# Six small re-orderings in a two-layer mixture-of-experts decoder trunk on one Trainium2 core

## The reference

```python
def reference(x, c, ...):
    cond = silu(c)
    h = x                                     # 512 tokens, 1024 channels
    for layer in range(2):
        mod = cond @ w_ada[layer] + b_ada[layer]
        sh1, sc1, g1, sh2, sc2, g2 = split(mod, 6)
        u = rms_norm(h, norm_mix[layer]) * (1 + sc1) + sh1
        if layer == 0:
            q, k, v, bg, cg, xv = split(u @ w_in)
            attn = sliding_window_attention(q, k, v, sinks)   # 8 heads of 64, window 128
            conv = bg * conv3(cg * xv)
            mix = concat(attn, conv) @ w_out
        else:
            mix = multiscale_pool_mixer(u, w_pool, pool_scale)
        h = h + g1 * mix
        u = rms_norm(h, norm_ffn[layer]) * (1 + sc2) + sh2
        h = h + g2 * grouped_moe(u, ...)      # 16 experts in 4 groups
    return rms_norm(h, norm_final)

def grouped_moe(...):
    # a token picks the best one of 4 groups, then the best 2 experts inside that group
    for e in range(16):
        out += gates[:, e] * ((silu(t @ w_gate[e]) * (t @ w_up[e])) @ w_down[e])
```

## Time and profile before

| | us |
|---|---|
| median of 3 runs | 782.37 (781.77 to 783.32) |
| profiled execution | 781.47 |
| its span | 779.6 |
| PE busy | 677.0 (87%) |
| DVE busy | 346.9 (44%) |
| ACT busy | 167.8 (22%) |
| POOL busy | 112.9 (14%) |
| transfers | 204.27 MB, 262 GB/s in the mean |

### The profile page before, as it was taken

One profiled execution on the slowest core, in us unless ns is written; L12 is line 12 of the kernel. 1 busy time (PEld: TensorE's weight loads), 2 busy tenths in 40 slices (PEclk: granted clock), 3 DMA queues, 4 the chain that ended last, 5 costly groups with the idle time before them and its releaser, 6 DMA issues. The chain is left out here.

```text
span 779.6 us, 7210 instructions
## 1 busy us (share of the span) xinstructions
PE 677.0 (87%) x2441; PEld 355.9 (46%) x2441; DVE 346.9 (44%) x623; ACT 167.8 (22%) x422; POOL 112.9 (14%) x87
## 2 busy tenths in 40 slices
PE   4899989999899955999999999179299999999960
PEld 2455434444444453455455454069255544554520
DVE  2226698999952356222232231336643223222312
ACT  4101121322212322121122121046022211211212
POOL 0000001001210032012212220100201222122020
PEclk8899999999999965999999999779589999999995
DMA  8999989978870376488888988525606889898326
GB/s 267 314 387 373 360 292 325 340 243 300 273 267 22 141 276 249 176 314 335 310 314 337 333 301 314 190 109 173 270 27 224 333 319 322 312 347 313 113 35 231
DMA packets 59930, 204.27 MB, mean 262 GB/s; under 512 B 13510, under 2 KB 22878, under 8 KB 47612
## 3 DMA queue, kind: packets, MB, share of 16 engines
q1 hardware_dynamic: 45012, 183.62, 62.1%
q0 software_dynamic: 10096, 19.45, 10.2%
q10 hardware_dynamic: 4792, 0.82, 0.6%
HBM read 193.06 MB, written 27.30 MB: 283 GB/s over the span
## 5 line engine op out<-in xcount | busy, mean ns | idle before, releaser
L1541 PE MATMUL ps<-ring,work 128*128 128x512 f32 x384 | 170.1, 596 | 0.0
L1541 PEld LDWEIGHTS ps<-ring,work 128*128 128x128 f32 x384 | 73.3, 192 | 90.7 <-issue 90.5
L844 DVE SCALAR_TENSOR_TENSOR acc<-adaw,cond,acc 128x1024 f32<-128x1024 f32 x70 | 97.4, 1391 | 10.1 <-DMA adaw<-in_w_ada_dram 8.2
L531 POOL DMA_INDIRECT h_dram<-work x32 | 50.6, 1581 | 309.0 <-DVE work L1159 285.3
L1140 DVE TENSOR_TENSOR work<-work,ps 128x256 f32<-128x256 f32 x32 | 13.5, 421 | 177.9 <-ACT work L753 177.8
L1564 PE MATMUL psY<-ring,work 128*128 128x512 f32 x192 | 86.6, 594 | 1.2 <-ACT work L763 1.2
L1396 PE MATMUL psY<-xu,ring 128*128 128x512 f32 x192 | 86.0, 601 | 0.0
L1159 DVE SCALAR_TENSOR_TENSOR work<-psY,work,gbc 128x512 f32<-128x512 f32 x64 | 45.1, 746 | 74.4 <-PE psY L1564 74.4
L753 ACT ACTIVATE work<-ps 128x256 f32<-128x256 f32 x32 | 12.3, 384 | 271.6 <-PE ps L1541 271.6
L1396 PEld LDWEIGHTS psY<-xu,ring 128*128 128x128 f32 x192 | 35.9, 192 | 45.4 <-issue 45.3
L747 ACT ACTIVATE work<-psA,modc,scl 128x128 f32<-128x128 f32 x120 | 45.2, 457 | 51.7 <-PE psA L1531 51.7
(11 more groups left out here) (183 smaller groups left out, 641.0 us busy)
## 6 DMA issues: line engine op xcount, KB each, us to landing
adaw<-in_w_ada_dram SPq DMA_DIRECT2D x84, 512.0 KB, 5.3
ring<-in_w_gate_dram SPq DMA_DIRECT2D x24, 1024.0 KB, 4.8
ring<-in_w_up_dram SPq DMA_DIRECT2D x24, 1024.0 KB, 7.0
ring<-in_w_down_dram SPq DMA_DIRECT2D x24, 1024.0 KB, 11.4
xu<-in_w_gate_dram SPq DMA_DIRECT2D x8, 1024.0 KB, 4.9
xu<-in_w_up_dram SPq DMA_DIRECT2D x8, 1024.0 KB, 7.0
xu<-in_w_down_dram SPq DMA_DIRECT2D x8, 1024.0 KB, 11.0
work<-in_w_ada_dram SPq DMA_DIRECT2D x12, 512.0 KB, 10.4
```

The source lines that it names most:

```text
L531: pool.indirect_dma_start(out=h_dram[l], out_offset=bass.IndirectOffsetOnAxis(tok_i[:, e:e + 1], 0), in_=yrow[:, e % 2, :], in_offset=None ...
L844: dve.scalar_tensor_tensor(total, adaw[:, n % ABUF, :], cond[:, k:k + 1], total if k else brow[:, :], ALU.mult, ALU.add).then_inc(mac_step, 1)
L1541: ins = pe.matmul(gu_ps[j % 2][:, :].rearrange("p (a f) -> p a f", a=2), xgT[:, j % 2, k, :], w_gu(j % 4)[:, :, k, :], start=(k == 0), sto ...
```

## The change

- The ten small loads leave ACT's queue for the head of POOL's program, behind a wait for the third `first_read`.
- One dummy matmul at the start instead of three.
- The first modulation sum (`ada_total(0)`, `ada_out(0)`) stands ahead of the attention units instead of inside the first.
- `scores` and `attend` alternate between the two halves of the array.
- The last eight experts are taken in the order 8, 12, 9, 13, 10, 14, 11, 15: SP loads their weights in that order, and the table's columns follow. Neighbours are of different groups from there on, so from the eleventh scatter of a layer on, a scatter waits for the one before the last.
- SP's second round of expert loads is written out. The loads of layer 1's first three experts stand behind the loads of h.

```diff
             def summed(i):
 
                 if i < 2:
-                    return 0
+                    return max(i, 0)
                 return NPC if i == len(PLACES) - 1 else sum(PLACES[:i - LAG + 1]) // KD
...
                 load_expert(l, 3, 3)
-                with sp.Fori(1, E // 4) as i:
+                for j in range(4):
+                    load_expert(l, 4 + j, j)
+                with sp.Fori(2, E // 4) as i:
                     for j in range(4):
-                        load_expert(l, 4 * i + j, j)
-                if l == 0:
-                    for e in range(3):
-                        load_expert(1, e, e)
+                        load_expert(l, 4 * i + j, j, 2 * i + 4 + j // 2 + 4 * (j % 2))
                 overflow_sync(sp, l)
 
                 for j in range(2):
                     sp.wait_ge(y_out[j], 8 * E * (l + 1))
                 for t in range(T):
                     sp.dma_start(h[:, t, :], h_dram[l][t * P:(t + 1) * P, :]).then_inc(h_back[t], 16)
+                if l == 0:
+                    for e in range(3):
+                        load_expert(1, e, e)
...
+            pool.wait_ge(first_read, PAIRS - 1)
+            for kv in range(KVH):
+                for odd in range(2):
+                    src = sinks[:, kv * GH + odd:(kv + 1) * GH:2].partition_broadcast(P).rearrange("p a e -> p (a e)")
+                    pool.dma_start(snk[:, 0, kv * GH + 2 * odd:kv * GH + 2 * odd + 2], src).then_inc(small_in, 16)
...
             load_gate(0, 0)
...
                 def scatter(e):
                     pool.wait_ge(y_ready, HEAD + l * E + e + 1)
-                    if e:
+                    if e > E // 2 + 1:
+
+                        pool.wait_ge(y_out[e % 2], 16 * (l * E // 2 + (e - 2) // 2 + 1))
+                    elif e:
 
                         pool.wait_ge(y_out[(e - 1) % 2], 16 * (l * E // 2 + (e - 1) // 2 + 1))
...
             for m in range(7):
                 empty(m)
+            for n in place_totals(1):
+                ada_out(n)
...
-            keep_clock(3, ps5[:, :])
+            keep_clock(1, ps5[:, :])
...
-                for g in range(GH):
+                for g in (0, 2, 1, 3):
...
-                for g in range(GH):
-                    odd, i = g // 2, g % 2
-                    dst = ps4[odd * HD:(odd + 1) * HD, (kv * 2 + i) * P:(kv * 2 + i + 1) * P]
+                for i in range(2):
                     for kb in range(0 if b else 1, 2):
-                        ins = pe.matmul(dst, vtok[:, b - 1 + kb, kv * HD:(kv + 1) * HD],
-                                        probT[:, kb, g * P:(g + 1) * P], start=(kb == 0 or b == 0), stop=(kb == 1))
+                        for odd in range(2):
+                            g = 2 * odd + i
+                            dst = ps4[odd * HD:(odd + 1) * HD, (kv * 2 + i) * P:(kv * 2 + i + 1) * P]
+                            ins = pe.matmul(dst, vtok[:, b - 1 + kb, kv * HD:(kv + 1) * HD],
+                                            probT[:, kb, g * P:(g + 1) * P], start=(kb == 0 or b == 0), stop=(kb == 1))
...
             project(6)
+            for n in place_totals(1):
+                ada_total(n)
...
                     for e in range(EPG):
-                        at0 = (n * EPG + e) * TC
+                        at0 = (len(TABLE[i]) * e + n) * TC
```

More of the change, by code:

```diff
@@ L382, in load_ada, with load_expert @@
                              [:, k]).then_inc(ada_in[n % ABUF], 16)
[L384 to L388, removed]
+            def load_expert(l, e, j, which=None):
+                which = e if which is None else which
+                gate = w_gate[l, bass.ds(which, 1)].rearrange("a (p k) f -> p (a k f)", k=KD)
+                up = w_up[l, bass.ds(which, 1)].rearrange("a (p k) f -> p (a k f)", k=KD)
+                down = w_down[l, bass.ds(which, 1)].rearrange("a (p c) d -> p (a c d)", c=2)
+                if not isinstance(which, int):
                     for s in (gate, up, down):
@@ L493, in load_gate @@
                                .rearrange("p a d -> p (a d)")).then_inc(gbc_in, 16)
+            pool.wait_ge(first_read, PAIRS - 1)
[3 more added lines that the diff above has]
+                    pool.dma_start(snk[:, 0, kv * GH + 2 * odd:kv * GH + 2 * odd + 2], src).then_inc(small_in, 16)
+            pool.dma_start(cvw[:, :, :], conv_w[0].rearrange("j (c p) -> p j c", p=P)).then_inc(small_in, 16)
+            pool.dma_start(wr[:, :, :], w_router.rearrange("(p k) e -> p k e", k=KD)).then_inc(small_in, 16)
+            pool.dma_start(brb[:, :], b_router.rearrange("(a e) -> a e", a=1).partition_broadcast(P)
+                           .rearrange("p a e -> p (a e)")).then_inc(small_in, 16)
+            for s in range(1, 4):
+                src = (norm_ffn if s % 2 else norm_mix)[s // 2]
+                src = src.rearrange("(k p) -> p k", p=P) if s == 2 else src.rearrange("(p k) -> p k", k=KD)
+                pool.dma_start(normc[:, s, :], src).then_inc(small_in, 16)
             load_gate(0, 0)
@@ L590, in _ @@
                           ).then_inc(vrow_in, 16)
[L591 to L603, removed]
             def ada_out(n):
```

## The result

| | before | after |
|---|---|---|
| median of 20 runs, us | 782.31 (780.53 to 791.38) | 779.58 (773.66 to 786.34) |
| ratio, 95% interval | | 0.9948 (0.9924 to 0.9973) |
| profiled execution, us | 781.47 | 773.66 |
| its span, us | 779.6 | 771.8 |
| PE / DVE / ACT busy, us | 677.0 / 346.9 / 167.8 | 670.5 / 346.4 / 167.4 |

The change saves half a per cent, 2.7 us of the 15.3 forecast by the medians. The ratio, which leaves out two slow executions of the change, says 4.1 us (2.1 to 5.9). The predicted 767.1 us and its range, 763.0 to 774.0, were **wrong**. The profiled execution of the change happens to be the lowest of its 20, so the two profiled executions alone would say 7.8 us, 5.1 too many.

What follows compares the result with a forecast made beforehand. PE bounds the expert stretches and DVE the attention units, so only start, first unit, layer border and end could give time: 6.2 + 1.6 + 1.7 + 0.8 + 5 = 15.3 us off 782.4, giving 767.1 us, range 763.0 to 774.0.

Steps and rivals of the forecast that it cites:

- The start: Kernel start: without small loads beside the first block, strips start 5 to 6 us earlier; 5 us saved, between 0 and 7.
- The price of the loads' return: Small loads back on POOL's queue at about 45 us: cost between nothing and about 4 us, put near the low end.
- What 5 us at PE are worth: Start: the first third of DVE's sums starts on first_read and shifts with PE; 5 us taken for the start.
- Moved weights: Layer border: nine weight loads behind h's four, 9.4 MB, are 26 us early for their first use; costed at nothing.
- The border: End of layer 0: scatter 15 starts at 494.5 instead of 500.71, and everything behind it moves as much; 6.2 us saved.
- Either half would take 4.6: Layer border: new scatter order or moved weights, each alone, would take 4.6 us; both together 6.2.
- The end: End of layer 1: scatter 15 starts at 757.2 instead of 758.83; 1.6 us saved.
- First sum and halves: Attention: early first sum removes DVE's 1.65 us wait, 1.7 us; alternating halves save 0.8 on the last two attends.
- The first: Rival: first block still lands at 21.0, start worth 1.9 to -2 us, time 770.2 to 774.1; chance 0.29.
- The second: Rival: two accumulating scatters in flight slow each other, 3.2 us less gain, 770.3; chance 0.05.
- The third: Rival: h's loads share with the nine weight loads, h lands 31 us after issue instead of 5.3, 793; chance 0.03.

Runs made afterwards that it cites:

- small_only: The kernel before with only the ten small loads moved to POOL's queue behind the third block: 788.86 us, ratio 1.0107.
- late_act: The changed kernel with its ten small loads on ACT's queue, behind ACT's first copy of modulation rows, none on POOL's: 773.67 us, ratio 0.9872.
- after_again: The changed kernel run and profiled once more, nothing edited: 780.69 us, ratio 0.9966.
- weights_only: The kernel before with only layer 1's first weights moved behind h: 784.42 us, ratio 1.0.
- scatter_only: The kernel before with only the last experts interleaved and the scatter's wait relaxed: 777.72 us, ratio 0.993.
- units_only: The kernel before with only the first modulation sum ahead of the attention units and scores and attend alternating between the halves: 781.04 us, ratio 0.996.
- small_on_act: The changed kernel with its ten small loads back in ACT's queue at their old place: 774.75 us, ratio 0.9906.
- late_ahead: late_act with layer 1's nine weight loads back ahead of the wait for the scatters: 773.81 us, ratio 0.9859.
- fours_on_pool: The changed kernel with six loads of 4-byte numbers on POOL's queue and the four long-row loads at ACT's old place: 777.44 us, ratio 0.9908.

## Why the prediction was wrong, step by step

Stage values below are means over the table's profiles that share the edit.

**The start: 5 us predicted, about -4.7 measured.** This is the step that failed. With the small loads at ACT's old place the start took 93.70 to 95.22, mean 94.3 (six profiles). With all ten on POOL's queue it took 96.63, 99.33 and 100.96, mean 99.0 (98.0 in the two profiles of the changed kernel itself). Two parts of my working were wrong.

- *The price of the loads' return*, "between nothing and what they cost in the 8 us of half rate, about 4 us", put near the low end. The bound came from the loads on ACT's queue, at half rate. On POOL's queue, with the 4-byte pieces among them, the same loads took the core down to 91 to 154 GB/s for 12 us, and to between 60 and 247 from 48 us on in the other two profiles. The row that I leaned on, POOL's column loads landing in 3.7 us, tells how fast such a load is for itself, not what it does to the stream beside it. small_only priced the move: 6.6 us slower where 5 faster had been expected.
- *What 5 us at PE are worth.* I let DVE's sums shift with PE. late_act has the strips 5.3 us earlier and no stretch near 100 GB/s, and its start is 92.25 (91.97 and 93.41 in its two relatives), in the mean 1.7 us less than 94.3. The wait of 5.28 us for a transfer in the earlier trace rows had already said that the stream of `w_ada` sets this stage. I had also left out that SP's next loads wait for PE's third `first_read`: a stream that runs ahead runs dry there, as small_only and after_again show.

The parts before that were right: first square, strips at 17.73, first block at 15.0, small loads no hindrance to L951 itself. I cited the Trainium skill (DMA: Bandwidth & Descriptors, Issuing engines are not separate DMA queues) as speaking against a gain. Its rule that all transfers share the same engines fits the loss in the 44 to 64 us stretch, while at 14 to 18 us taking the small loads away did speed up the first block, from 187 to 400 GB/s. That another issuing engine saves only issue time is not what the runs show: the same ten loads cost the core 2.2 to 2.6 MB from ACT and 3.7 to 5.1 MB from POOL.

**Moved weights: nothing predicted, 3 us measured.** I looked for a late store or gather and found 26 us of cover, which held. The cost lay elsewhere, in PE's clock during the head, which I had not asked about. The head took 53.5 to 53.7 us in the five profiles with the weights ahead, and 53.2 to 58.1, mean 56.3, in the eight with them directly behind h. That eats what the move gives at the border. weights_only, at 1.0, settles that the edit is worth nothing here. Why the clock is lower there is open: in after_again the transfers run at 416 GB/s in the mean between 512 and 536 us, well before the last product at 545.24, and two of eight profiles escaped. One of these two is the first profile of the very kernel that after_again repeats.

**The border: 6.2 predicted, 5.4 measured.** The mechanism was right. Scatter 15 starts 2.17 us behind DVE's last rows as I had it (1.41 + 0.8), but its own issue took 2.49 us instead of 1.55 and h was asked for 7.14 us behind it, not 6.27. "Either half would take 4.6": scatter_only gave 4.2, weights_only 3.0.

**The end: 1.6 predicted, 1.7 measured.** Experts 1 fell from 172.90 to 173.01 to between 171.00 and 171.35 in every kernel with the new order.

**First sum and halves: 1.7 + 0.8 = 2.5 predicted.** units_only's ratio gives 3.1 us, interval 1.1 to 5.2. The halves do run together: an attend takes 1.09 us instead of 1.58, which saves 0.98 us on the two on the path, while the 48 larger score products stayed at 6.8 us. The Trainium skill (TensorEngine Tiling, Key Properties) lets different tiles run in parallel; the trace shows it for the attends' pairs, by 31% and not by half. The stage from L943 to the first gather took 202.67 to 205.73 with the old code (five profiles, mean 204.3) and 201.44 to 203.59 with the new (nine, mean 202.4), which says 1.9.

**The sum.** By stage means: start -4.7, units 1.9, border 5.4, head -2.8 (against 53.5), end 1.7: 1.5 us, and the medians say 2.7. With the start of the changed kernel's own two profiles, -3.7, it is 2.5. Against the 15.3 the start explains 9.7 and the head 2.8 of the difference.

**The rivals.** The first, that the start gives little, was nearest, but its floor of -2 was not low enough. The second fell: two scatters do overlap, at the cost above. The third fell: the first tile of h was there 3.6 us after its issue (501.47 to 505.06), and the transfers of h in both layers landed after 5.1 us in the median, against 5.3 before.

## What to carry to other kernels

Before moving transfers off a busy engine's queue, ask what they will do to the stream that runs where they land, and price that by size of the single piece: ten loads with a few thousand 4-byte pieces cost more on GpSimd's queue than the ACT time that they freed. Ask too whether the stream's own issuer waits further on for the engine that was to be sped up. Where a stage's last wait is for a transfer, time won at its compute start does not come out at its end. Of this change the best cut that was run keeps the new expert order, the sum, the halves and the short clock warm-up, and issues the small loads from ACT behind the first block's work: 773.7 us (ratio 0.987) with layer 1's weights behind h or ahead of it. Against small_on_act, which leaves the small loads where they were (774.75, 0.9906), that is not clear of the noise: the intervals overlap.

## What the runs showed that was not expected

- Small loads of 4-byte pieces: on ACT's queue 187 GB/s beside them at the start and 207 to 218 at 30 to 40 us in late_act and late_ahead; on POOL's queue 60 to 66 GB/s over 4 us in after_again and fours_on_pool. The page of queues, before and then after (packets, MB, share of the 16 engines' time), does not count the pieces alike on the two queues:

```profile
q0 software_dynamic: 10096, 19.45, 10.2%
q10 hardware_dynamic: 4792, 0.82, 0.6%
```
```profile
q0 software_dynamic: 10432, 19.55, 11.1%
q10 hardware_dynamic: 536, 0.73, 0.3%
```

  ACT's queue (q10) loses 4256 packets and 0.3% of the engines' time. The queue that carries POOL's loads (q0) gains only 336 packets, but 0.9%. By these shares the same loads keep the engines busy two to three times as long there, which is an estimate, since the queue carries other transfers too. Why is not shown.

- A scatter issued 5.2 us behind another took 2.49 us on POOL in layer 0 and 1.55 in layer 1, so its own neighbour is not the reason. DVE is at work beside it in layer 0, but that can't be all: in scatter_only and late_ahead, with DVE at the same work, it took 1.80. The cause stays open.
- Full clock over the last narrow products of a stage is not certain: the same 32 products took 3.65 us in late_ahead and 6.85 in late_act, which differ only in where nine transfers stand, and 3.64 and 5.95 in two executions of one kernel (after and after_again).
